# PEER experts in a hybrid decoder step: 16 more tokens on gathered expert rows

## The reference

```python
q = (x @ lp['peer_wq']).reshape(N, PEER_HEADS, 2, PEER_DHALF)
s = jnp.einsum('nhcd,ckd->nhck', q, lp['peer_subkeys'])
v1, i1 = lax.top_k(s[:, :, 0], PEER_TOPK)
v2, i2 = lax.top_k(s[:, :, 1], PEER_TOPK)
cand = (v1[..., :, None] + v2[..., None, :]).reshape(N, PEER_HEADS, 256)
sc, ci = lax.top_k(cand, PEER_TOPK)
idx = take(i1, ci // 16) * N_KEYS + take(i2, ci % 16)
gate = jax.nn.softmax(sc, axis=-1)
hid = jnp.einsum('td,thkd->thk', x, peer_u[idx])
hid = gelu(hid) * gate
out = jnp.einsum('thk,thkd->td', hid, peer_v[idx])
```

## Time and profile before

| | us |
|---|---|
| median of 3 runs | 2627.42 |
| lowest, highest | 2625.96, 2630.22 |
| the profiled execution, its own time | 2625.02 |
| its span | 2623.6 |
| stages to the close | 0 to 1010 |
| pick | 1024 to 1336 |
| spread | 1336 to 1540 |
| experts | 1540 to 2609 |
| store | 2609 to 2624 |

### The profile page before, as it was taken

The page is one execution under the profiler, slowest core; times in us unless marked ns, Lnnn a source line. Parts: engine busy times, 40 slices in busy tenths (PEclk is TensorE's granted clock), DMA queues, the critical chain, the costliest instruction groups (busy, mean ns, idle before and its releaser), DMA issues. The chain is left out here.

```text
span 2623.6 us, 44929 instructions
## 1 busy us (share of the span) xinstructions
PE 2349.6 (90%) x16971; PEld 2064.1 (79%) x16971; DVE 1738.9 (66%) x3598; ACT 768.1 (29%) x1303; POOL 965.9 (37%) x651
## 2 busy tenths in 40 slices
PE   2999888888869897999989979999999998999898
PEld 2899777766543596776668859998999998999888
DVE  2662555454567342899769827777777778888785
ACT  1422111121322221112257733332333333333331
POOL 2000000000013000223300037887888877888782
PEclk8999888998568798999989989999999999999999
DMA  2223000211248321222316897776777776887781
GB/s 69 72 88 114 14 3 3 58 56 58 65 133 287 127 89 58 60 79 79 119 59 176 219 328 281 271 278 246 265 278 260 281 263 242 289 298 281 265 295 33
DMA packets 252157, 428.95 MB, mean 163 GB/s; under 512 B 81029, under 2 KB 181824, under 8 KB 237281
## 3 DMA queue, kind: packets, MB, share of 16 engines
q1 hardware_dynamic: 206433, 264.20, 31.3%
q0 software_dynamic: 45568, 162.63, 17.0%
HBM read 383.10 MB, written 43.68 MB: 163 GB/s over the span
## 5 line engine op out<-in xcount | busy, mean ns | idle before, releaser
L2447 PE MATMUL experts_pV<-experts_GH,experts_VH 128*128 128x392 f32 x1024 | 370.1, 361 | 16.8 <-DVE keep_xT L2608 16.8
L2563 POOL TENSOR_TENSOR experts_VL<-experts_V,experts_VH 128x2048 fp32r<-128x2048 f32 x64 | 296.6, 4635 | 169.2 <-ACT experts_VH L2491 168.9
L2447 PE MATMUL experts_pV<-experts_GL,experts_VH 128*128 128x392 f32 x1024 | 350.4, 342 | 0.0
L2447 PE MATMUL experts_pV<-experts_GH,experts_VL 128*128 128x392 f32 x1024 | 350.3, 342 | 0.0
L2608 DVE TENSOR_TENSOR keep_xT<-experts_pV,keep_xT 128x392 f32<-128x392 f32 x512 | 273.7, 554 | 23.1 <-PE experts_pV L2447 22.9
L2434 PE MATMUL experts_pH<-keep_xh,experts_UH 128*128 128x392 f32 x704 | 241.6, 343 | 0.0
L2434 PE MATMUL experts_pH<-keep_xl,experts_UH 128*128 128x392 f32 x704 | 240.2, 341 | 0.0
L2434 PE MATMUL experts_pH<-keep_xh,experts_UL 128*128 128x392 f32 x704 | 239.5, 340 | 0.0
L1260 POOL IOTA att_dist<- 128x528 f32 x1 | 0.6, 572 | 630.1 <-POOLq L73 630.1
L2447 PEld LDWEIGHTS experts_pV<-experts_GH,experts_VH 128*128 128x128 f32 x1024 | 194.6, 190 | 30.1 <-DVE keep_xT L2608 28.7
L2485 ACT ACTIVATE experts_UH<-experts_pU 128x512 fp32r<-128x512 f32 x176 | 105.0, 597 | 366.7 <-PE experts_pU L2422 366.7
(11 more groups left out here) (432 smaller groups left out, 5335.1 us busy)
## 6 DMA issues: line engine op xcount, KB each, us to landing
experts_V<-in_peer_v SPq DMA_DIRECT2D x64, 1024.0 KB, 6.0
experts_U<-in_peer_u SPq DMA_DIRECT2D x44, 1024.0 KB, 7.6
scratch_gates<-spread_M SPq DMA_DIRECT2D x3, 7680.0 KB, 35.6
experts_M<-scratch_gates SPq DMA_DIRECT2D x64, 360.0 KB, 3.1
keep_K<-in_cache_k SPq DMA_DIRECT2D x64, 256.0 KB, 3.5
keep_V<-in_cache_v POOLq DMA_DIRECT2D x64, 256.0 KB, 3.9
front_w<-in_w_in SPq DMA_DIRECT2D x30, 512.0 KB, 3.8
pick_U<-in_peer_u SPq DMA_DIRECT2D x24, 512.0 KB, 3.8
```

The costliest lines, as they stand in the source:

```text
L2447: last = nc.tensor.matmul(pV[n % 4][:, 0:DT], l, r, start=(t == 0), stop=(t == 5))
L2563: nc.gpsimd.tensor_tensor(VL[q.b][:, :, :], V[q.b][:, :, :], VH[q.b][:, :, :].bitcast(F32), ALU.subtract).then_inc(v_lo, 1)
```

## The change

16 more tokens (`WIDE`) leave the dense way, so `DT` is 376 in place of 392. They use gathered rows too, but with one row for each head and token: 8 heads x 16 tokens fill the 128 partitions, and 16 gathers (one for each of a head's picks) serve them, so `K` is 144. Their tokens' values are put on the partitions by one copy, eight transposes and two copies (`xw`), and their sums (`yw`) are added over the heads in the store by a matmul with `head`.

In pick the four units are 125, 125, 126 and the 128 sparse tokens, and all heads of the 16 tokens make one more unit, chosen once behind the heads; a small copy `q16` on ACT ahead of each query copy collects their queries. In spread the tiles are 120, 120, 104 and 32 tokens, 94 units, and `STEPS`, the units to a hidden block, is 7 in place of 8. In the store there are six tiles: four of 94, 128 and 16.

```diff
-DT = TQ - SPARSE
-NJ = TT - 1
-WD = DT // NJ
+WIDE = 16
+DT = TQ - SPARSE - WIDE
+UNITS = [(0, 125), (125, 125), (250, 126), (DT, SPARSE)]
-SPREAD = [(0, 120), (120, 120), (240, 120), (360, 32)]
+SPREAD = [(0, 120), (120, 120), (240, 104), (344, 32)]
...
-                    for j in range(TT):
-                        last = nc.tensor.matmul(pS[0:w, 2 * j + e, :], qT[:, e, j * WD:j * WD + P], kT[:, e, :],
-                                                start=True, stop=True)
+                    for j, (t0, n) in enumerate(UNITS):
+                        last = nc.tensor.matmul(pS[0:w, 2 * j + e, :], qT[:, e, t0:t0 + P], kT[:, e, :], start=True, stop=True)
...
+            def score_wide():
+                for e in range(2):
+                    last = nc.tensor.matmul(pS[0:w, 2 * UN + e, :], q16[:, e, :, :].rearrange("p h t -> p (h t)"), kT[:, e, :],
+                                            start=True, stop=True)
...
+                sc(nc)(q16[:, e, h, :], acc[:, 1, h2 - WIDE:h2], ACT.Copy)
                 sc(nc)(halves3(qT[:, e:e + 1, :]), acc[:, :, 0:h2], ACT.Copy).then_inc(queried, 1)
...
-            sc(nc)(ex[:, :, 2, :, :], ex[:, :, 2, :, :], ACT.Exp).then_inc(expd, 1)
+            sc(nc)(ex[:, :, 2, :, :], ex[:, :, 2, :, :], ACT.Exp)
+            sc(nc)(exw[:, :, 2, :], exw[:, :, 2, :], ACT.Exp).then_inc(expd, 1)
             act.wait_ge(turned, 1)
             for q in range(3):
-                sc(nc)(eT[:, q, :].rearrange("p (j t) -> p j t", j=NJ), pS[:, q * NJ:(q + 1) * NJ, 0:WD], ACT.Copy).then_inc(taken, 1)
+                for j, (t0, n) in enumerate(UNITS[:-1]):
+                    sc(nc)(eT[:, q, t0:t0 + n], pS[:, 3 * q + j, 0:n], ACT.Copy).then_inc(taken, 1)
...
-            for h in range(PH):
-                g = h % 2
-                if h + 1 < PH:
+            for h in range(PH + 1):
+                g, u = h % 2, units(h)
+                if h < PH:
                     best_of_halves(h + 1)
...
-    K = PH * TOPK
+    KS = PH * TOPK
+    K = KS + TOPK
...
+                pe.wait_ge(x_each, 1)
+                for b in range(2):
+                    for k in range(4):
+                        each = yw[:, (4 * b + k) * P:(4 * b + k + 1) * P]
+                        last = nc.tensor.transpose(pV[2 + b][:, k * P:(k + 1) * P], each, c["ident"][:, :])
+                    last.then_inc(x_turned, 1)
...
+            x, y = (xs, ys) if n % K < KS else (xw, yw)
             if n < K:
-                nc.vector.scalar_tensor_tensor(out=row[n % SLOTS], in0=row[n % SLOTS], scalar=1.0, in1=xs[:, :],
+                nc.vector.scalar_tensor_tensor(out=row[n % SLOTS], in0=row[n % SLOTS], scalar=1.0, in1=x[:, :],
...
-STORED = [(j * WD, WD) for j in range(NJ)] + [(DT, SPARSE)]
+STORED = [(94 * j, 94) for j in range(DT // 94)] + [(DT, SPARSE), (DT + SPARSE, WIDE)]
...
+                if j == LAST:
+                    pe.wait_ge(heads, 1)
+                    nc.tensor.matmul(pt[n % 4][0:w, :, :], head[:, :], yw[:, 512 * half:512 * half + 512].rearrange("p (q d) -> p q d", q=4),
+                                     start=True, stop=False)
                 for q in range(4):
-                    last = nc.tensor.transpose(pt[n % 4][0:w, q, :], acc[:, 4 * half + q, t0:t0 + w], c["ident"][:, :])
+                    x = acc[:, 4 * half + q, t0:t0 + w]
+                    if j < LAST:
+                        last = nc.tensor.transpose(pt[n % 4][0:w, q, :], x, c["ident"][:, :])
+                    else:
+                        last = nc.tensor.matmul(pt[n % 4][0:w, q, :], x, c["ident"][:, :], start=False, stop=(q == 3))
```

More of the change, by code:

```diff
@@ L1851, in peer_choose @@
     h2 = TQ // 2
+    UN = len(UNITS)
+    units = lambda h: UN if h < PH else 1
     wv = ins["peer_wq"][0].rearrange("(c p) n -> p c n", p=P)
@@ L2059, in _ @@
             look(PH // 2 - 1, 0)
+            pairs(PH // 2, 0, 1)
             look(PH // 2 - 1, 1)
+            look(PH // 2, 0, 1)
         @blk.vector
@@ L2084, in best_of_halves @@
                 dve.wait_ge(copied, h + 2)
-                for j in range(TT):
-                    top16([(v[g][:, j, e, :], ix[:, j, e, :], S[g][:, 2 * j + e, :], S2[e][:, :]) for e in range(2)])
+                scores = S[g] if h < PH else Sw
+                for j in range(units(h)):
+                    top16([(v[g][:, j, e, :], ix[:, j, e, :], scores[:, 2 * j + e, :], S2[e][:, :]) for e in range(2)])
             def indices(h):
-                nc.vector.tensor_copy(ixf[h % 2][:, :, :, :], ix[:, :, :, :]).then_inc(halved, 1)
+                nc.vector.tensor_copy(ixf[h % 2][:, 0:units(h), :, :], ix[:, 0:units(h), :, :]).then_inc(halved, 1)
                 dve.wait_ge(halved, h + 3)
@@ L2441, in product_v @@
                 pe.wait_ge(g_lo, q.count(2, 2))
-            if not q.after(1) and n < 2:
+            if not q.after(1) and n < 4:
                 pe.wait_ge(x_rows, n + 1)
@@ L2519, in first @@
                     sc(nc)(xh[:, k, :], xn[:, k, 0:DT], ACT.Copy).then_inc(x_hi, 1)
-                for b in range(2):
+                for b in range(4):
                     act.wait_ge(x_turned, b + 1)
-                    sc(nc)(xs[:, b * 512:(b + 1) * 512], pV[b][:, :], ACT.Copy).then_inc(x_rows, 1)
+                    to = (xs if b < 2 else xw)[:, b % 2 * 512:(b % 2 + 1) * 512]
+                    sc(nc)(to, pV[b][:, :], ACT.Copy).then_inc(x_rows, 1)
                 for st in range(4):
@@ L2673, in _ @@
         def _(pe):
-            for n in range(2 * TT):
+            for n in range(2 * N):
                 j, half = n // 2, n % 2
@@ L2684, in _ @@
         def _(dve):
-            for n in range(2 * TT):
+            nc.vector.tensor_reduce(head[:, :], c["ident"][:, :].rearrange("p (h t) -> p t h", h=PH), AX.X, ALU.add).then_inc(heads, 1)
+            for n in range(2 * N):
                 j, half = n // 2, n % 2
@@ L2703, in _ @@
                 sp.dma_start(outs["y_prompt"][0, t0:t0 + prompt, :], rows[j % 2][0:prompt, :]).then_inc(stored[j % 2], 16)
-            sp.dma_start(outs["y_sample"][:, 0, :], rows[NJ % 2][SPARSE - DEC:SPARSE, :]).then_inc(stored[NJ % 2], 16)
-            sp.wait_ge(stored[0], 64)
-            sp.wait_ge(stored[1], 32)
+            sp.dma_start(outs["y_sample"][:, 0, :], rows[LAST % 2][WIDE - DEC:WIDE, :]).then_inc(stored[LAST % 2], 16)
+            for b in range(2):
+                sp.wait_ge(stored[b], 16 * (N // 2) + 16 * (b == LAST % 2))
 def hybrid_step(nc, ins, outs, scr):
```

130 lines of the change are left out of this document (81 added, 49 removed).

## The result

The changed kernel takes 2697.26 us (median of 6; 2693.55 to 2700.39) against 2627.69 before (median of 6): a ratio of 1.0267, 95% interval 1.0251 to 1.0282. The forecast was 2616 in a range of 2594 to 2645, so the change went the other way, and past the range. Its profiled execution took 2699.48 us, with a span of 2697.5 in place of 2623.6.

| us | before | after | moved | forecast |
|---|---|---|---|---|
| pick | 311.6 | 304.5 | -7.1 | -6.0 |
| spread | 204.0 | 200.4 | -3.6 | -2.4 |
| experts | 1069.0 | 1129.3 | +60.3 | -27.5 |
| store | 14.9 | 38.0 | +23.1 | +25 |

The account below looks back on a forecast made before the run. TensorE was taken to bound experts, 1069 of 2624 us. Experts -27.5, pick -6.0, spread -2.4 and store +25 summed to -10.9 us, giving a forecast of 2616 us, range 2594 to 2645.

Parts of the forecast that it names:

- What bounds: Experts is set by TensorE, little room on VectorE and GpSimd; pick by hidden blocks; store by its DMA-copy-DMA chain.
- Narrower matmuls: Experts: 5184 matmuls of 376 columns in place of 392, 7.3 ns less each, 1.75 us a cycle, -37.7 us in all.
- More rows, late cycles: Experts after the turn: two more rows cost 1.35 us a cycle, leaving -0.4 each, -4 us over ten cycles.
- Catches: Experts: row multiplies held some 8 us around VL; three taken from the rounding in place of four, -6.7 us.
- The first: Rival: more catches in late 7/7/1 cycles of experts, 6.7 us each; four give +20, 2647 us; chance 0.15.
- The rival of the store (not slowed): Store: the two-engine reading of 94-row stores fails, the sixth tile costs 1.5 us; 2592 us; chance 0.09.
- Pick, spread, store: Terms of three stages: pick -6.0 us, spread -2.4 us, store +25 us from 94-row stores over two engines.
- The choice's saving: Pick: choosing experts loses 7 of 40 units, about 41 us of VectorE, none reaching the end behind 20 hidden blocks.
- The chance of slower, 0.19: Whole kernel above 2632.7 us: 0.15 from late-cycle catches, 0.03 from the weight load, 0.01 besides.

Follow-up runs that it names:

- e4: Changed kernel with the 16 tokens' gathers and row multiplies left out, so they get no experts: 2610.41 us.
- e10: Kernel before the change, with row multiplies placed as in e8: 2573.23 us, ratio 0.9801.
- e8: Changed kernel with e1's store tiles, rows 7/7/1, multiplies before an early pair's gates and otherwise mostly in VectorE's waits: 2556.25 us, ratio 0.9740.
- e2: Changed kernel with the row multiplies ahead of an early pair put before its two gates: 2614.05 us.
- e3: Changed kernel without the seventh gather of any pair (16 gathers left out, all multiplies kept): 2627.27 us.
- e5: Changed kernel with late rows dealt 6/6/3 in place of 7/7/1, multiplies standing where they stood: 2681.56 us.
- e6: Kernel before the change, with the row multiplies ahead of an early pair put before the two gates: 2597.11 us, ratio 0.9892.
- e1: Changed kernel with store tiles of 128, 128, 120, 128 and 16 tokens in place of four of 94, 128 and 16: 2674.44 us.
- e7: Changed kernel with the edits of e1, e2 and e5 together: 2593.20 us, ratio 0.9886.
- e9: As e8, but with late rows dealt 6/6/3: 2563.24 us in a single run.

## Why the prediction was wrong, point by point

**What bounds.** Right for pick, the store and experts ahead of the turn: PE's hidden blocks, the chain of transfers and PE's pace set them. Behind the turn PE was busy 82 to 85 of 100 us and waited for DVE.

**Narrower matmuls.** Right, by the pace: 0.179 to 0.171. As a gain it was a little large: 0.5 of 1.75 us a cycle did not arrive (e4). Between e10 and e8, where PE waits for nothing in the early cycles, it came nearly whole: 46.3 to 44.7. The Trainium skill ("Perfetto Trace Analysis", Identifying the Most-Contended Engine) names the weight load's busy share, beside the share of the peak rate that the matmuls reach, as what tells TensorE's headroom. Read by the 96.9% in the earlier trace rows alone there was no such room; the runs show that for these matmuls there was, so the measurement decides.

**More rows, late cycles.** This is the step that failed: "I take 1.35, as both are at 83 to 84%". It priced two rows as work, 1.35 us a cycle, and they cost 12 (57.9, against 47.67 less the 1.75 of the columns). The 0.46 for one row came from one cycle with a seventh gather in its second pair only the earlier trace rows. With one in both, VL begins 0.01 to 0.02 us after a gather in both, the first multiply is held 5.53 and brings DVE late to the second. e2 shows 8.3 of the 12 as the early pair's multiply, e3 that both holds follow the gathers, e5 that the multiply's place decides. The term counted work of DVE and GpSimd, and had nothing for the clock of PE, whose slower work makes up some 3 of the 12.

**Catches.** The mechanism was right and the count wrong: "I take three" by the rounding alone, eleven came, eight of them in the late cycles (2140 to 2546), seven of those at pairs with one row. The three taken from the rounding (1800, 2039, 2603) did come, and so did the fourth, left out (2546). The price of 6.7 was near (7.1 in e6, 8.3 in e2), in part by luck: it was DVE's held time, 8.00 less 1.3, taken as PE's. Behind the four of the kernel before PE waited 4.5 to 6.1 us, and lost about 2 more in the 6.8 us at a granted clock of 0.50.

**The rivals.** The first was what happened, at twice the number that it was priced at. What spoke against it, "a VL delayed by a seventh gather met none", was read from that same single cycle; in it the multiply nearest ahead of that VL began 3.3 us sooner and was over. A mechanism that needs two instructions to meet within 0.5 us can't be dismissed, or counted, from one cycle when the change moves both. That the cycles repeat could be read before: the early ones without a catch lie between 47.4 and 47.6. What meets in one 7/7/1 cycle was likely to meet in all, so its price belonged to all of the late cycles, not to four. The rival of the store (not slowed) fell with the stage of 38.0 us, and e1 shows why.

**Pick, spread, store.** -7.1, -3.6 and +23.1 against -6.0, -2.4 and +25. The choice's saving did not reach the end: DVE waits 36 us longer, near the 41 of the sum. A 94-row store takes 7.3 us, just under the lower bound of 7.5, so a packet's 0.16 us was the right end.

**Range and chances.** The upper end, 2645, left out eight catches. The chance of slower, 0.19, was that of four chance meetings, not of a rhythm.

## What to carry to other kernels

Where two engines can hold each other, work that is added to a loop shifts its rhythm, and a meeting that happens once in the loop can happen every time, as in the eight late cycles here: look for the pairs of instructions that come near each other, and place them, before counting work. A long instruction of VectorE with two SBUF operands belongs where GpSimd is in gathers that no long instruction follows at once, and where VectorE waits anyway; placing alone gave the kernel before 2.0% (e10). When a tile of rows changes its size, see what the new row count divides by before it is stored.

## What the runs showed of the hardware

A multiply with two SBUF operands that begins on VectorE 0.04 to 0.5 us ahead of VL loses to it where GpSimd goes from a gather to VL without a gap (0.02 us), and then takes 7.6 to 8.0 us in place of 1.27: it comes through only behind VL and two GL. Two other cases went the other way. At 2090.10, where GpSimd had been idle, VL began 0.15 us into a multiply, the multiply took 1.28, and VL 5.61 in place of 4.6. And multiplies that began 0.7 to 0.9 us ahead of a VL without a gap took 1.27 to 1.29 and stretched VL to 4.8 to 5.0 (eight of them, in e2, e5, e7, e8 and e9).

An unbroken row on GpSimd does not always hold to its end. The changed kernel has 31 multiplies that begin inside a VL which had started after a gap behind a gather. They take 1.5 to 2.5 us and come through behind VL alone, and the first GL takes 2.0 in place of 1.0. The eight of 5.5 us began inside a VL straight behind a gather, and stayed behind both GL. Why the start of VL decides this is not shown.

Operations with one operand in PSUM were not held: none of the 816 adds, gates and UL in experts of the changed kernel took over 0.70 us. The Trainium skill ("SBUF — State Buffer", SBUF: two separate sides) tells that the two engines share a port pair, that an instruction of VectorE with two SBUF inputs contends for it with a GpSimd instruction that reads SBUF, and that the one that starts first has it for the whole instruction. The runs agree on which instructions are held and on the full hold. That the first has it does not hold behind a gather, by the rows above, and a hold can last three instructions.

After a wait of PE of 5.6 us (2264.13) the granted clock stood at 0.50 for 6.8 us, so that what holds VectorE cost PE more than the wait. In e9 the same wait of 1.8 us was followed by 3.4 us at 0.50 in some cycles and by none in others.

94 rows of 4 KB went out over two engines in 7.3 us, 128 rows over 16 (e1). The same skill ("DMA: Bandwidth & Descriptors", Why a DMA increments its semaphore by 16 and not by 1) has the rule, the largest number up to 16 that divides the rows on both sides, and the stores read here agree: 14 for 98, 2 for 94, 16 for 128, 15 for 120, 8 for 8.
